# Hyena stage of a two-block kernel: fourfold split of signal spectra and inverse, two filter-spectrum buffers, part of the products on GpSimd

## What is computed

```python
def hyena_mixer(xn, ...):
    p = xn @ w_in + b_in                      # 3 x 1024 channels
    p = conv_b + sum(pp[:, j:j + L] * conv_w[j] for j in range(3))
    x1, x2, v = jnp.split(p, 3, axis=-1)
    kf = jnp.fft.rfft(hyena_filters(L, ...), axis=0)     # filters normed by sum |k|
    z = v
    for o, gate in enumerate((x1, x2)):
        z = gate * (long_conv(z, kf[:, o]) + fbias[o] * z)
    return z @ w_out + b_out

def long_conv(u, kf):
    U = jnp.fft.rfft(u, n=2 * L, axis=1)
    return jnp.fft.irfft(U * kf[None], n=2 * L, axis=1)[:, :L]
```

## Time and profile before

| | us |
|---|---|
| median of 3 runs | 4452.47 (4443.47 to 4454.98) |
| span of the profiled execution, first to last instruction | 4437.2 |
| TensorE matmul busy | 4169.9 (94%) |
| VectorE / ScalarE / GpSimd busy | 2225.3 / 1236.0 / 1445.5 |
| four convolution passes of layer 0 (197 to 435) and of layer 3 (2098 to 2334) | 238 and 236 |

### The profile page before, as it was taken

The page is one execution under the profiler, slowest core; times in us unless marked ns, Lnnn a source line. Parts: engine busy times, 40 slices in busy tenths (PEclk is TensorE's granted clock), DMA queues, the critical chain, the costliest instruction groups (busy, mean ns, idle before and its releaser), DMA issues.

```text
span 4437.2 us, 48379 instructions
## 1 busy us (share of the span) xinstructions
PE 4169.9 (94%) x19126; PEld 3108.9 (70%) x19126; DVE 2225.3 (50%) x3267; ACT 1236.0 (28%) x1725; POOL 1445.5 (33%) x834
## 2 busy tenths in 40 slices
PE   7999999999999699999999999989998999998999
PEld 6656888656788488877557887566666666685887
DVE  6567435365424652465774444556663357404322
ACT  3322212135222322233233222322322224422221
POOL 3311344200344144434123442357574000231343
PEclk9999999999999899999999998989999879999999
DMA  6200232210232123221003222121212121221232
GB/s 181 76 16 23 111 105 88 105 48 28 101 115 77 70 96 118 81 77 67 28 29 131 99 90 68 43 60 31 60 30 57 59 77 60 74 95 62 90 105 76
DMA packets 96913, 333.75 MB, mean 75 GB/s; under 512 B 44336, under 2 KB 47536, under 8 KB 67888
## 3 DMA queue, kind: packets, MB, share of 16 engines
q1 hardware_dynamic: 87968, 311.85, 20.2%
q10 hardware_dynamic: 8720, 18.82, 1.7%
HBM read 317.53 MB, written 13.11 MB: 75 GB/s over the span
## 4 chain that ended last, share of the span: by engine, by line
PE 80%; DVE 14%; ACT 2%; POOL 2%; issue 1%; DMA 0%; SPq 0%; DVEq 0%; ACTq 0%; POOLq 0%
PE bank L903 16%; PE bank L904 16%; PE bank L905 16%; PE bank L1340 5%; PE bank L867 4%; PE bank L1107 3%; PE bank L1057 2%; PE bank L1320 1%; PE bank L1641 1%; PE bank L1081 1%; PE bank L1640 1%; PE bank L1662 1%; PE bank L1572 1%; PE bank L1601 1%; DVE work L2598 1%
## 5 line engine op out<-in xcount | busy, mean ns | idle before, releaser
L782 POOL TENSOR_TENSOR w_lo<-ring,w_hi 128x2048 fp32r<-128x2048 f32 (+2 forms) x200 | 777.2, 3886 | 1509.6 <-ACT w_hi L1777 1483.1
L903 PE MATMUL bank<-x_hi,w_hi 128*128 128x512 f32 x1584 | 618.2, 390 | 7.5 <-POOL w_lo L782 7.5
L905 PE MATMUL bank<-x_hi,w_lo 128*128 128x512 f32 x1584 | 616.9, 389 | 0.0
L904 PE MATMUL bank<-x_lo,w_hi 128*128 128x512 f32 x1584 | 616.7, 389 | 0.0
L1777 ACT ACTIVATE w_hi<-ring 128x2048 fp32r<-128x2048 f32 (+2 forms) x200 | 322.0, 1610 | 712.8 <-PE bank L905 711.9
L903 PE MATMUL bank<-h_hi,w_hi 128*128 128x512 f32 x960 | 373.9, 389 | 0.4
L904 PE MATMUL bank<-h_lo,w_hi 128*128 128x512 f32 x960 | 373.5, 389 | 0.0
L905 PE MATMUL bank<-h_hi,w_lo 128*128 128x512 f32 x960 | 373.4, 389 | 0.0
L903 PEld LDWEIGHTS bank<-x_hi,w_hi 128*128 128x128 f32 x1584 | 297.8, 188 | 70.6 <-POOL w_lo L782 9.2
L905 PEld LDWEIGHTS bank<-x_hi,w_lo 128*128 128x128 f32 x1584 | 297.6, 188 | 62.1
L904 PEld LDWEIGHTS bank<-x_lo,w_hi 128*128 128x128 f32 x1584 | 297.8, 188 | 61.5
(11 more groups left out here) (468 smaller groups left out, 7666.1 us busy)
## 6 DMA issues: line engine op xcount, KB each, us to landing
ring<-stream SPq DMA_DIRECT2D x212, 1024.0 KB, 4.8
ring<-stream SPq DMA_DIRECT2D x64, 704.0 KB, 4.0
ring<-stream SPq DMA_DIRECT2D x36, 512.0 KB, 3.6
xn<-first_mods SPq DMA_DIRECT2D x8, 1024.0 KB, 6.9
ring<-stream SPq DMA_DIRECT2D x4, 1088.0 KB, 5.0
bias_rows<-work ACTq DMA_DIRECT2D x1, 4096.0 KB, 46.4
work<-bias_rows ACTq DMA_DIRECT2D x1, 3072.0 KB, 11.2
tab<-tabs ACTq DMA_DIRECT2D x1, 2624.0 KB, 16.8
```

The costliest lines, as they stand in the source:

```text
L782: nc.gpsimd.tensor_tensor(w_lo[:, j % 2, 0:cols], ring[:, k % RING, 0:cols], w_hi[:, j % 2, 0:cols], ALU.subtract).then_inc(wlo_set, 1)
L903: mm(b[:], hi[:, at + k, :], rhs_hi, start=(k == 0), stop=False)
L904: mm(b[:], hi[:, at + k, :], rhs_lo[:, k, :], start=False, stop=False)
L905: ins = mm(b[:], lo[:, at + k, :], rhs_hi, start=False, stop=(k == kt - 1))
```

## The change

Tokens are split by t mod 4 (`r:T:4`) and not by parity. A signal spectrum is then eight matmuls of one term each in place of sixteen, joined in two levels: `signal_pair` out of PSUM into `U` and `partner` (`ctmp`), then a difference and a sum of four rows each. The inverse takes two terms of 128 columns per residue r in place of four of 256 per parity, and the products are joined in two levels before it. Filter spectra stay at sixteen matmuls. Filter spectra go to `xn` and a new tensor `spectrum2` in turn, so those of pass i + 1 are made in pass i. Channels 0 to 383 of 512 (`SHARE`) are multiplied by VectorE, the last 128 by GpSimd (`multiply`, fourteen stepped operations); TensorE waits for `pool_prod_set` ahead of the fourth tile of the inverse. The magnitudes' scratch is x itself, which is written to memory at the start of the layer and read back in pass 2, both by ScalarE's queue. Work on `taps`, transposes and decays is moved to other places, `low_z` of the first half to behind the products. The scratch size for dynamic DMA is set to 1024. The core of the diff:

```diff
+SHARE = 384
...
+        spectrum2 = sb("spectrum2", [P, 8, 512])
...
+        mags, mags2 = x[:, 0:4, :], x[:, 4:8, :]
+        partner = ctmp.rearrange("p a b c -> p (a b) c")
+        cross = TB("cross").rearrange("p (g c) -> p g c", g=4)
+        cross2 = kbuf2[:, 0:4 * (512 - SHARE)].rearrange("p (g c) -> p g c", g=4)
...
+                def multiply(i):
+                    t = n["signal"] + 21 * i
+                    pool.wait_ge(aux_drained[t % BANKS], t // BANKS + 1)
+                    tt = nc.gpsimd.tensor_tensor
+                    sig, ker, a, b = U[:, :, SHARE:], K[i % 2][:, :, SHARE:], partner[:, :, SHARE:], cross2
...
+                    step(tt(sig[:, 4:8], sig[:, 0:4], a, ALU.subtract))
+                    step(tt(sig[:, 0:4], sig[:, 0:4], a, ALU.add))
+                    ur, us, kr, ks = sig[:, 0:8:2], sig[:, 1:8:2], ker[:, 0:8:2], ker[:, 1:8:2]
+                    step(tt(a, us, ks, ALU.mult))
+                    step(tt(b, ur, ks, ALU.mult))
...
+                    tt(sig[:, 6:8], b[:, 0:2], b[:, 3:1:-1], ALU.subtract).then_inc(pool_prod_set, 1)
...
+                decay(0)
+                decay(1)
+                for i in range(4):
+                    multiply(i)
+                    if i < 2:
+                        decay(i + 2)
+                    if i == 2:
+                        for b in range(2):
+                            low_weights(first + 18 + b, out_hi[b])
...
+                def signal_spectra():
+                    for t in range(n["turned"] - 4, n["turned"]):
+                        pe.wait_ge(aux_drained[aux.place(t)], aux.turn(t) + 1)
+                    for pair in SIGNAL_PAIRS:
+                        for kind, r in pair:
+                            mm(open_aux()[:], fwd[kind, r, 1], u_tm[:, r, :], start=True, stop=True).then_inc(aux_full, 1)
...
+                def inverse_tile(b, ct, r):
+                    for k in range(2):
+                        ins = mm(b[:, P * r:P * (r + 1)], U[:, INVERSE_SLOTS[r][k], ct * P:(ct + 1) * P], inv[:, r, k, :],
+                                 start=(k == 0), stop=(k == 1))
+                    return ins
+                def inverse(i):
+                    full_ = acc_full if i < 3 else aux_full
+                    tiles = [open_acc() if i < 3 else open_aux() for _ in range(3)]
+                    pe.wait_ge(prod_set, n["prod"] + 1)
+                    for ct in range(3):
+                        inverse_tile(tiles[ct], ct, 0)
+                        inverse_tile(tiles[ct], ct, 2)
+                    pe.wait_ge(prod_set, n["prod"] + 2)
+                    for ct in range(3):
+                        inverse_tile(tiles[ct], ct, 1)
+                        inverse_tile(tiles[ct], ct, 3).then_inc(full_, 1)
+                    n["prod"] += 2
+                    b = open_acc() if i < 3 else open_aux()
+                    pe.wait_ge(pool_prod_set, n["prod"] // 2)
+                    for r in range(3):
+                        inverse_tile(b, 3, r)
+                    inverse_tile(b, 3, 3).then_inc(full_, 1)
...
                 filter_spectra()
+                magnitudes()
+                taps_of(1, w3)
                 pe.wait_ge(conv_done, 24 * (s + 1))
+                turns(0)
                 for i in range(4):
...
+                    signal_spectra()
                     if i < 3:
...
+                        filter_spectra()
+                        magnitudes()
+                        turns(i + 1)
                     else:
                         begun = first_half(0) + first_half(1)
...
+                    if i == 0:
+                        pe.wait_ge(*later[0])
+                    if i < 2:
+                        taps_of(i, later[1])
+                    inverse(i)
...
+                act.dma_start(x_keep.rearrange("(k p) t -> p k t", p=P), x[:]).then_inc(hy_x_out, 16)
...
+                taps()
                 act.wait_ge(conv_done, n["conv"])
+                turned()
                 for i in range(4):
-                    o, c = i // 2, i % 2
+                    spectra(4)
                     if i < 3:
...
+                        magnitudes()
+                        spectra(4)
+                        aux.n += 1
+                        turned()
+                    if i == 2:
+                        act.dma_start(x[:], x_keep.rearrange("(k p) t -> p k t", p=P)).then_inc(hy_x_back, 16)
+                        for j in range(2):
+                            high_weights(starts[("hyena", s)] + 18 + j, out_hi[j])
                     if i == 3:
                         for m in range(4):
                             high_z(m)
-                    spectra(4)
+                        act.wait_ge(aux_full, aux.n)
+                        high_weights(starts[("hyena", s)] + 20, out_hi[2])
+                    for ct in range(2):
+                        scaled_rows(i, ct)
+                    if i < 2:
+                        taps()
+                    for ct in range(2, 4):
+                        scaled_rows(i, ct)
+                        if i == 3:
+                            high_z(4 + ct - 2)
...
+                    mine = slice(0, SHARE)
+                    sig, ker, a, b = U[:, :, mine], K[c][:, :, mine], partner[:, :, mine], cross
...
+                    signal_pair(0, U[:, 0, :], U[:, 2, :])
+                    signal_pair(1, U[:, 1, :], U[:, 3, :])
+                    signal_pair(2, partner[:, 0, :], partner[:, 3, :])
+                    signal_pair(3, partner[:, 1, :], partner[:, 2, :], True)
+                    tt_(sig[:, 4:8], sig[:, 0:4], a, ALU.subtract)
+                    step(tt_(sig[:, 0:4], sig[:, 0:4], a, ALU.add))
                     if i < 3:
+                        filter_pair(next_, 0)
+                    tt_(a, us, ks, ALU.mult)
+                    step(tt_(b, ur, ks, ALU.mult))
+                    if i < 3:
+                        filter_pair(next_, 1)
+                        magnitudes()
+                    tt_(ur, ur, kr, ALU.mult)
+                    step(tt_(us, us, kr, ALU.mult))
+                    if i < 3:
+                        filter_pair(next_, 2)
+                    tt_(ur, ur, a, ALU.subtract)
+                    step(tt_(us, us, b, ALU.add))
+                    if i < 3:
+                        filter_pair(next_, 3)
+                        norms(1 - c)
+                    tt_(a, sig[:, 0:4], sig[:, 4:8], ALU.add)
+                    step(tt_(b, sig[:, 0:4], sig[:, 4:8], ALU.subtract))
+                    tt_(sig[:, 0:2], a[:, 0:2], a[:, 2:4], ALU.add)
+                    signal(tt_(sig[:, 4:6], a[:, 0:2], a[:, 2:4], ALU.subtract), prod_set)
+                    tt_(sig[:, 2:4], b[:, 0:2], b[:, 3:1:-1], ALU.add)
+                    signal(tt_(sig[:, 6:8], b[:, 0:2], b[:, 3:1:-1], ALU.subtract), prod_set)
+                    if i < 3:
+                        aux.n += 4
+                    if i < 2:
                         acc.n += 8
-                    aux.n += 4
                     if i == 3:
                         for m in range(4):
                             low_z(m)
...
+                        y = bank(t, i == 3)[:].rearrange("c (r h) -> c h r", r=4)
+                        drain(stt(mid, y, invn[:, m:m + 1], mid, ALU.mult, ALU.add), t, i == 3)
+                        signal(tt_(z, zbias[:, ct % 2, :], hy[:, 8 * (i // 2) + m, :], ALU.mult), gated)
...
+                dve.wait_ge(hy_x_back, 16 * (s + 1))
...
+            def filter_pair(dst, j):
+                even, odd, t = pair_tiles(j)
+                tt_(dst[:, j, :], even, odd, ALU.add)
+                drain(tt_(dst[:, j + 4, :], even, odd, ALU.subtract), t, True)
```

More of the change, by code:

```diff
@@ L821, in hyena @@
+                n["signal"] = n["aux"] + 3 + 13 + 7
+                decay(0)
[7 more added lines that the diff above has]
+                            low_weights(first + 18 + b, out_hi[b])
+                for b in range(2, 4):
                     low_weights(first + 18 + b, out_hi[b])
+                n["aux"] += 3 + 4 * (1 + 8 + 4 + 8) + 4
@@ L1010, in hyena @@
                 pe.wait_ge(stack_set, s + 1)
-                taps = [weights()]
-                taps_of(0, taps[0])
+                w3 = weights()
+                taps_of(0, w3)
                 blk.take()
@@ L1016, in hyena @@
                 blk.take()
-                taps.append(weights_later())
+                later = weights_later()
                 blk.take()
@@ L1038, in hyena @@
-                    last = aux.n - 1
-                    for t in range(last - 3, last + 1):
-                        pe.wait_ge(aux_drained[aux.place(t)], aux.turn(t) + 1)
-                    spectra(lambda kind: u_tm, (0, 1))
-                    if i < 3:
-                        n["filt"] += 4
-                        pe.wait_ge(filt_set, n["filt"])
-                        spectra(lambda kind: filt[:, kind], (0,))
+                        filter_spectra()
+                        magnitudes()
```

(61 more changed lines are left out.)

193 lines of the change are left out of this document (75 added, 118 removed).

## The result

| | us |
|---|---|
| kernel before, median of 4 runs taken beside the changed one | 4453.73 (4443.47 to 4457.34) |
| changed kernel, median of 4 runs | 4506.45 (4505.77 to 4510.52) |
| ratio | 1.0119, 95% interval 1.0105 to 1.0134 |
| span of the profiled execution of the changed kernel | 4508.7 |

The change makes the kernel slower by 1.2%, 53 us by the medians. The forecast was 8 us faster, its range ended at 4477, and 0.28 stood on slower.

A forecast was written before the change was run, and what follows sets the result against it. TensorE bounds the stage, then VectorE's chain: first T at 215.9 plus 52.9 + 52.9 + 56.0 + 53.9 gives 431.6 against 435.4, 7.6 us off two layers, about the same off median 4452.5: 4444.9 us, range 4400 to 4477.

The forecast's parts named there:

- What bounds the kernel, and that VectorE's chain takes over: Hyena passes: TensorE bounds now, its work falls from 55 to 42 us a full pass, then VectorE's chain is longer.
- the entries at fences only: GpSimd enters only at VectorE's fences: 2 x 0.9 us before the products are set, at T + 30.5.
- T: The last signal pair of a pass on VectorE, from which times are counted; first at 215.9 us in layer 0.
- Passes 0 and 1: First two passes of a layer: 52.9 us each from one last signal pair to the next.
- The price of a turn, 0.9: Blocking of VectorE by each big 512-column GpSimd product operation, taken from the earlier trace: 0.9 us.
- Pass 2: Third pass: two low weight halves of 4.2 us blocking each fall on gatings; next last signal pair after 56.0 us.
- Pass 3: Last pass: products end 25.4 us after the last signal pair, first half behind them, last low half at 53.9.
- Parking x at nothing: Writing x to memory and reading it back costs nothing; at most up to 23 us once a layer.
- The sum: Layer 0's last low half ends at 431.6 in place of 435.4: 3.8 us a layer, 7.6 in all.
- Rival (a), strict alternation: GpSimd also enters between unfenced VectorE operations: 15 us slower over two layers, 4467.5 us; chance 0.30.
- Rival (b): GpSimd's share costs VectorE nothing: 70 us faster, 4382 us; chance 0.12.
- (c): Split doesn't shorten the inverse, or x's transfer holds up the ring: 4465 to 4490 us; 0.13 including stalls missed.

## Why the prediction was wrong, point by point

**What bounds the kernel, and that VectorE's chain takes over.** Right. TensorE's work fell, VectorE is busy 51 of 57 us, the products are 1.76 alone and about 2.7 beside GpSimd, and a decay that meets a short operation costs it some 2 us, as the earlier trace rows had it.

**The share's cost: the entries at fences only.** This is the step that failed in every pass. The prediction held that an unfenced follower leaves no gap because it starts before the former ends; L2600 does start early and takes 2.83. In pass 0, by the excess of each row over its price alone, GpSimd's turns cost the ten big products 7.1 us, the maximum 1.0 and the last small product 2.2 (a decay), 10.3 in place of the 1.8 assumed; the second `prod_set` came at T + 39.1 and not T + 30.5. About half was given back: the readings, charged 11.3 us with GpSimd beside them, took 7.1 since GpSimd was nearly done. Passes 0 and 1 end 3.8 and 3.5 us late.

**The price of a turn, 0.9.** Too low: 1.07. Ten turns differ by 1.7 us.

**Pass 2.** 5.4 us late. The two low weight halves were put on gatings, but fell on the last two small products (5.16 and 5.24 us in place of 0.95), ahead of the second `prod_set`, with TensorE waiting:

```profile
383.33 5.16 DVE L2621 TENSOR_TENSOR work<-tab 128x768 f32<-128x768 f32 x1
388.41 5.24 DVE L2622 TENSOR_TENSOR work<-tab 128x768 f32<-128x768 f32 x1
```

**Pass 3.** 11.0 us late. The products ended at T + 32.5, which is the rival's T + 32, not the T + 25.4 of fences only: 7.1 us. From there to the inverse's start (461.59) 15.1 became 19.5, since low weights blocked `low_z` by 4.6 us; the inverse and the readings took 0.5 less than assumed.

**Parking x at nothing.** Right as a transfer and wrong as an instruction, and with 19.3 us the largest single term in layer 0. The prediction looked for a price in the DMA's share and the ring's lead; it didn't ask how long the issue itself holds ScalarE. The first T came at 235.2 and not 215.9: 17.3 us by the held issue, 2.0 mostly by the taps at half clock (8.93 us in place of 7.12). With the issue moved, T comes at 214.4. Its upper bound of 23 us a layer had the size right, in one layer of the two.

**The sum.** For layer 0: -3.8 as forecast, +17.3 +2.0, and +3.8 +3.5 +5.4 +11.0 in the four passes give +39.2; the trace has +39.05.

**Rival (a), strict alternation.** This is what happened, and 0.30 was too little for it: the evidence against was the absence of a row, not a row. Even (a) was 12 us a layer short (227 against 239.3 for the four passes), for the price of a turn, the turn taken at the maximum, the decays on the small products and the low weights ahead of `prod_set`. Rival (b) was wrong, and of (c) the split is as short as it says (the inverse took 7.31 us where 8.2 was assumed), while x did cost time, but through ScalarE and not through the ring.

**The point from which it pays.** The prediction said that all that is laid on VectorE is paid in full. Ten turns of 1.07 and four of about 0.5 hold VectorE for 12.7 us where all fall under its operations; what GpSimd took off it is ten times 0.53 and four times 0.27, 6.4. Where the turns fall under VectorE's operations the share doesn't pay, and all on VectorE is indeed 24 us faster.

## What to carry to other kernels

Where VectorE and GpSimd both work on two inputs in SBUF, count each GpSimd operation on VectorE's side nearly in full (here its length less 0.2 us), fenced or not, and compare that with what the share takes off; give GpSimd the stretches in which VectorE reads PSUM or waits, and make it wait for them by a semaphore rather than start when its data are there. The issue of a DMA is an instruction of its engine and can hold it, 18.84 us here right behind a 4 MB transfer on the same queue: look at its length in the trace, and put it where the queue is free. Before speeding up an engine off the path, ask which other engine's work it will start sooner, and on what that will fall.

## What the runs showed of the hardware that was not expected

- A DMA issue on ScalarE's queue 2.2 us behind a 4 MB transfer took 18.84 us (18.80 to 18.87 in six kernels), the same issue took 0.37 to 0.39 us in three other places, and one on SyncE's queue took 0.33 us in the meantime.
- An unfenced VectorE operation starts 0.09 us before the former one ends and yet lets a waiting GpSimd operation in between: 2.83 us in place of 1.75. The Trainium skill ("SBUF — State Buffer", Who interferes with whom) has whoever comes first hold the pair for its whole instruction; the trace agrees with that, and shows beside it that with both waiting the two take turns.
- A turn's price goes with the length of GpSimd's operation: 1.07 us for one of 1.27 alone, 0.53 for one of 0.73, and 2.05 to 2.15 for a decay of 2.33 (1.22 became 3.27 and 3.37), each about 0.2 less than the length.
